# Hybrid decoder layer: the low halves of attention's gate weights made by a negated copy and an accumulating transfer

## What is computed

```python
h = x + 0.5 * swiglu(rmsnorm(x), w_gate_up1, w_down1)
u = rmsnorm(h)
xp | q | k | v | gate_logits = u @ w_in
y_pool = causal_pool_mixer(xp) @ w_branch_pool
y_sb = stick_breaking_attention(q, k, v) @ w_branch_attn
g_pool, g_sb = split(sigmoid(gate_logits))
h = h + (g_pool * y_pool + g_sb * y_sb) @ w_out
h = h + 0.5 * swiglu(rmsnorm(h), w_gate_up2, w_down2)
out = rmsnorm(h)
```

## Time and profile before

| | |
|---|---|
| median of 3 runs | 1924.63 us (1923.79 to 1924.80) |
| profiled execution | 1924.49 us |
| its span in the profile | 1922.5 us |
| PE busy | 1911.0 us (99%) |
| VectorE busy | 1392.9 us (72%) |
| ScalarE busy | 786.7 us (41%) |
| GpSimd busy | 152.1 us (8%) |
| granted TensorE clock | full throughout |

### The profile page before, as it was taken

How to read it: one execution, slowest core, us unless ns; L and a number is a source line. 1 busy time by engine, 2 the same in 40 slices (tenths; PEclk the granted TensorE clock), 3 DMA queues, 4 the chain that set the end, 5 groups by cost and what they waited for, 6 DMA issues and landing times.

```text
span 1922.5 us, 25204 instructions
## 1 busy us (share of the span) xinstructions
PE 1911.0 (99%) x9046; PEld 1599.3 (83%) x9046; DVE 1392.9 (72%) x1714; ACT 786.7 (41%) x1170; POOL 152.1 (8%) x221
## 2 busy tenths in 40 slices
PE   9999999999999999999999999999999999999998
PEld 9888888888888888888888888898888888888886
DVE  6977867774566776786878878879777777755655
ACT  7423232323434543345665652464323232334344
POOL 1000000000000300002443420010000000000002
PEclk9999999999999999999999999999999999999999
DMA  5456654558676534248446347643545444677665
GB/s 165 147 198 228 225 174 149 189 196 312 210 236 196 185 110 151 73 134 236 142 127 175 105 154 254 191 136 114 182 141 197 148 168 153 220 265 240 204 195 200
DMA packets 246723, 347.19 MB, mean 181 GB/s; under 512 B 16368, under 2 KB 150256, under 8 KB 243056
## 3 DMA queue, kind: packets, MB, share of 16 engines
q1 hardware_dynamic: 246640, 346.10, 55.3%
HBM read 232.79 MB, written 112.98 MB: 180 GB/s over the span
## 4 chain that ended last, share of the span: by engine, by line
PE 95%; DVE 2%; DMA 1%; ACT 1%; issue 1%; POOL 1%; SPq 0%; POOLq 0%; DVEq 0%; ACTq 0%
PE bank L1233 39%; PE bank L1330 10%; PE bank L1277 8%; PE bank L1278 8%; PE bank L1279 8%; PE bank L1187 5%; PE bank L1471 4%; PE bank L1379 2%; PE bank L1407 2%; PE bank L1437 2%; PE bank L1543 2%; PE bank L1162 1%; PE bank L1562 1%; PE bank L1561 1%; PE bank L1528 1%; PE bank L1526 1%
## 5 line engine op out<-in xcount | busy, mean ns | idle before, releaser
L2171 DVE TENSOR_TENSOR dn_lo<-dn_lo_raw,dn_hi 128x1024 fp32r<-128x1024 f32 x149 | 181.9, 1223 | 150.9 <-ACT dn_hi L1741 150.5
L1233 PE MATMUL bank<-lo_t,wa_hi 128*128 128x512 f32 x640 | 249.0, 389 | 0.0
L1233 PE MATMUL bank<-hi_t,wa_hi 128*128 128x512 f32 x640 | 249.0, 389 | 0.0
L1233 PE MATMUL bank<-hi_t,wa_lo 128*128 128x512 f32 x640 | 249.0, 389 | 0.0
L1741 ACT ACTIVATE dn_hi<-dn_lo_raw 128x1024 fp32r<-128x1024 f32 x149 | 157.9, 1060 | 219.3 <-DMA dn_lo_raw<-act_dram 219.3
L1277 PE MATMUL bank<-dn_hi 128*128 128x512 f32 x596 | 232.5, 390 | 0.0
L1279 PE MATMUL bank<-dn_lo,dn_hi 128*128 128x512 f32 x596 | 231.9, 389 | 0.0
L1278 PE MATMUL bank<-dn_hi,dn_lo 128*128 128x512 f32 x596 | 231.9, 389 | 0.0
L1233 PE MATMUL bank<-hi_b,wa_hi 128*128 128x512 f32 x480 | 186.9, 389 | 0.9 <-DVE up L2295 0.9
L1233 PE MATMUL bank<-lo_b,wa_hi 128*128 128x512 f32 x480 | 186.8, 389 | 0.0
L1233 PE MATMUL bank<-hi_b,wa_lo 128*128 128x512 f32 x480 | 186.7, 389 | 0.0
(11 more groups left out here) (275 smaller groups left out, 3764.1 us busy)
## 6 DMA issues: line engine op xcount, KB each, us to landing
wa_lo_raw<-in_ffn_w_gate_up_dram SPq DMA_DIRECT2D x87, 512.0 KB, 4.9
dn_lo_raw<-act_dram SPq DMA_DIRECT2D x149, 256.0 KB, 4.3
act_dram<-g SPq DMA_DIRECT2D x44, 512.0 KB, 4.3
wd_t<-in_ffn_w_down_dram SPq DMA_DIRECT2D x44, 512.0 KB, 6.6
act_dram<-s_of SPq DMA_DIRECT2D x88, 256.0 KB, 6.4
wd_dram<-wd_t SPq DMA_DIRECT2D x22, 1024.0 KB, 5.9
dn_lo_raw<-wd_dram SPq DMA_DIRECT2D x85, 256.0 KB, 3.4
dn_lo_raw<-in_ffn_w_down_dram SPq DMA_DIRECT2D x64, 256.0 KB, 3.1
```

The lines of the kernel that those rows point to most:

```text
L1233: last = nc.tensor.matmul(acc, lhs, rhs, start=n == 0 and i != 2 and i < 5, stop=n == 11, skip_group_check=True)
L2171: return nc.vector.tensor_tensor(dst, raw, hi.bitcast(f32), ALU.subtract)
```

## The change

ScalarE makes, right after each high half, the negated high half: a copy of the raw weights with scale -1 into `w_lo`, which is rounded in the same way. When the fourth piece of a unit is done, GpSimd issues one transfer of the whole unit, 128 by 2048 elements or 1 MB, from `w_raw` onto `w_lo`, with addition as its accumulating operation, so that `w_lo` becomes raw less high. Its completion raises `wsum` by 16. VectorE's 28 subtractions go. PE waits at the third matmul of a unit for `wsum` (unit 0 still for `wlo`), and SP waits for `wsum` before it loads over `w_raw`, one step later than before. `wghi` and `wglo`, of the pool's group weights, become one semaphore; no instruction moves by that. `lows_before` counts the low halves that VectorE still makes.

```diff
+def lows_before(g):
+    return min(g, U_GATE + 1) + max(g - U_C, 0)
...
                 if gg >= 2:
                     sp_.wait_ge(whi, gg - 1)
-                    sp_.wait_ge(wlo, gg - 1)
+                    if U_GATE < gg - 2 < U_C:
+                        sp_.wait_ge(wsum, 16 * (gg - 2 - U_GATE))
+                    else:
+                        sp_.wait_ge(wlo, lows_before(gg - 1))
...
-                    for j, piece in PIECES_AT[s - 2] if s > 1 else ():
+                    for j, piece in PIECES_AT[s - 3] if s > 2 else ():
...
                     if m == 2 and fb == GATE_FIRST[j]:
-                        pe.wait_ge(wlo, U_GATE + j + 1)
+                        if j:
+                            pe.wait_ge(wsum, 16 * j)
+                        else:
+                            pe.wait_ge(wlo, U_GATE + 1)
...
                 ab, kts = 2 * piece // PIECES, slice(KT // 2 * (piece % 2), KT // 2 * (piece % 2 + 1))
-                nc.scalar.activation(w_hi[:, par, ab, kts, :], w_raw[:, par, ab, kts, :],
-                                     ACT.Copy).then_inc(whi if piece == PIECES - 1 else wpiece, 1)
+                nc.scalar.activation(w_hi[:, par, ab, kts, :], w_raw[:, par, ab, kts, :], ACT.Copy)
+                last = nc.scalar.activation(w_lo[:, par, ab, kts, :], w_raw[:, par, ab, kts, :], ACT.Copy, scale=-1.0)
+                if piece == PIECES - 1:
+                    last.then_inc(whi, 1)
...
-                for j, piece in PIECES_AT[s - 1] if s else ():
-                    split_piece(j, piece)
...
+            def add_weights(j):
+                par = j % 2
+                pool.wait_ge(whi, U_GATE + j + 1)
+                if j > 1:
+                    pool.wait_ge(wsum, 16 * (j - 1))
+                nc.gpsimd.dma_start(w_lo[:, par].rearrange("p a k f -> p (a k f)").bitcast(f32),
+                                    w_raw[:, par].rearrange("p a k f -> p (a k f)"), accum_op=ALU.add).then_inc(wsum, 16)
+
             for s in range(NA + DRAIN):
+                for j, piece in PIECES_AT[s - 1] if s >= 1 else ():
+                    if piece == PIECES - 1:
+                        add_weights(j)
                 if s < NA:
                     mask_diagonal(s)
```

More of the change, by code:

```diff
@@ L459, in macaron_layer @@
         wlo = sem("wlo")
-        wpiece = sem("wpiece")
-        wghi = sem("wghi")
-        wglo = sem("wglo")
+        wsum = sem("wsum")
+        wg_split = sem("wg_split")
         mb_in = sem("mb_in")
@@ L1027, in load_branch_unit @@
                 sp_.wait_ge(whi, g - 1)
-                sp_.wait_ge(wlo, g - 1)
+                if n < 2:
+                    sp_.wait_ge(wsum, 16 * (g - 2 - U_GATE))
+                else:
+                    sp_.wait_ge(wlo, lows_before(g - 1))
                 for k in range(0, BR, 2):
@@ L1104, in _ @@
             sp_.wait_ge(whi, U_C + 1)
-            sp_.wait_ge(wlo, U_C + 1)
+            sp_.wait_ge(wlo, lows_before(U_C + 1))
             for b in range(2):
@@ L1388, in group_quad @@
                 pe.wait_ge(ylo, 2 * m + 2)
-                pe.wait_ge(wglo, 1)
+                pe.wait_ge(wg_split, 2)
                 for b in range(4):
@@ L1591, in branch_tile @@
                 pe.wait_ge(whi, U_C + j + 1)
-                pe.wait_ge(wlo, U_C + j + 1)
+                pe.wait_ge(wlo, lows_before(U_C + j + 1))
                 for th in (1, 0) if j == 0 else (0, 1):
@@ L2028, in _ @@
             act.wait_ge(mb_add, 5 * NM)
-            nc.scalar.activation(wg_hi[:, :, :], wg_raw[:, :, :], ACT.Copy).then_inc(wghi, 1)
+            nc.scalar.activation(wg_hi[:, :, :], wg_raw[:, :, :], ACT.Copy).then_inc(wg_split, 1)
             pool_hi(0, 1)
@@ L2706, in group_weights_lo @@
             def group_weights_lo():
-                dve.wait_ge(wghi, 1)
+                dve.wait_ge(wg_split, 1)
                 nc.vector.tensor_tensor(wg_lo[:, :, :].rearrange("p g d -> p (g d)"),
@@ L2711, in group_weights_lo @@
                                         wg_hi[:, :, :].rearrange("p g d -> p (g d)").bitcast(f32),
-                                        ALU.subtract).then_inc(wglo, 1)
+                                        ALU.subtract).then_inc(wg_split, 1)
             def pool_weight_sums(u):
@@ L2881, in turned_lo @@
                                             at_hi[:, kbs, c0:c0 + P].bitcast(f32), ALU.subtract).then_inc(alo, 1)
[L2883 to L2894, removed]
             for s in range(NA + DRAIN):
```

## The result

| | before | after |
|---|---|---|
| median, us | 1924.53 (1923.79 to 1925.33) | 1929.61 (1927.37 to 1930.48) |
| executions | 13 | 13 |
| ratio, 95% interval | | 1.0025 (1.0016 to 1.0033) |
| profiled execution, us | 1924.49 | 1929.00 |
| its span, us | 1922.5 | 1927.2 |

The changed kernel is slower by 5.1 us, a ratio of 1.0025. The forecast was 1927.0 us and no change that can be told; the time lies inside the range of 1923 to 1940, but 2.6 us above the forecast and just past the 0.2% that divides "no change" from "slower", which the interval still includes. The mechanism came as forecast at one place, and a second place was missed. When the changed kernel was timed again (e7), one execution of twelve ran at a mean granted clock of 0.752 and took 2386.57 us; it is left out of the median given there.

What follows compares the result with a forecast made beforehand. The prediction took TensorE (PE), busy 1911.0 of 1922.5 us, as the bound. From 1924.49 us, less 0.4 for VectorE, plus 0 for ScalarE and 2.75 for unit 7's wait, it reached 1926.84, given as 1927.0; range 1923.0 to 1940.0.

Steps and rivals of the forecast that it cites:

- What bounds it, and what is removed: Attention stage: PE bounds and waits only 1.28 us; removing VectorE's 28 subtractions gives back 0.4 us.
- ScalarE's copies at 0: ScalarE's 28 negated copies add 0.53 us each, but idle time or other work hides them: cost 0.
- The transfer's length: Accumulating 1 MB transfer from GpSimd's queue: 6.0 us as a plain one plus 2.4 for the second operand, 8.4 us.
- Unit 7: At unit 7 the lead time is 5.65 us against 8.4 us of transfer, so PE waits 2.75 us.
- Units 1 to 6 at nothing: At the six other units lead times of 8.66 us or more cover the transfer, so PE waits nothing.
- Slow transfer: Rival: sums landing from 9.3 us on make several units wait and the kernel slower, 1939.4 us at 12.0; chance 0.34.
- Starved descriptors: Rival: GpSimd can't write the transfer's descriptors while VectorE runs, so sums come after 10.97 us; 1933.0 us, chance 0.10.
- Hidden: Rival: the transfer takes under 5.65 us and PE never waits for it; 1923.4 to 1924.2 us, chance 0.14.
- The sign: Whole kernel: no change that can be told, within 0.2% or 3.85 us, 0.52; slower 0.44, faster 0.04.

Runs made afterwards that it cites:

- e1: The changed kernel without its seven transfers, and with nobody waiting for one; 1924.57 us, ratio 1.0003.
- e4: The changed kernel with plain transfers in place of accumulating ones, same queue, size, source and target; 1924.69 us, ratio 1.0003.
- e5: The changed kernel with four transfers of 256 KB a unit, each as soon as ScalarE has made its piece; 1925.31 us, ratio 1.0005.
- e9: As e5, but GpSimd issues the additions of units 1 to 6 behind the step's masks, not ahead; 1926.16 us, ratio 1.0012.

## Why the prediction was right, and where it was wrong

- **What bounds it, and what is removed:** right in kind. PE gained almost nothing from VectorE's 28 instructions. The place of the earlier trace rows gave back 0.19 to 0.20 us, where 0.4 was taken.
- **ScalarE's copies at 0:** right as a sum, wrong in one place. At unit 2 the piece at 928.56 of the earlier trace rows had no idle time behind it: `at_hi` started 0.57 us after it before, and starts 1.04 us after it now (the piece's high half is at 929.84). VectorE's low half and its scan follow `at_hi`, and PE's transposes step by 0.26 us. ScalarE there, before and in the changed kernel:

```profile
929.13 0.28 ACT L2092 ACTIVATE at_hi<-bank 128x128 fp32r<-128x128 f32 x1
```

```profile
930.36 0.63 ACT L2129 ACTIVATE w_lo<-w_raw 128x512 fp32r<-128x512 f32 x1
930.88 0.28 ACT L2107 ACTIVATE at_hi<-bank 128x128 fp32r<-128x128 f32 x1
```

  That ate the 0.2 us that VectorE gave back, which is why e1 shows no gain. "Nearly every piece is followed by idle time" was read from a few places; the piece that PE's chain ran through was the one to look at.
- **The transfer's length:** right. Taken as 6.0 + 2.4 = 8.4 us; measured 8.0, and its parts are 5.4 plain and 2.6 for the addition, one less and one more than taken. The fit in the Trainium skill, "DMA: Bandwidth & Descriptors", section "Anatomy of one DMA — SWDGE (gpsimd) path", gave 4.4 us for the plain megabyte; e4 measured 5.4. The estimate made from that page with 2 MB read, 6.8, was low as well. Here the measurement decides.
- **Unit 7:** right, and so close by some luck. The lead of 5.65 us stood; the issue came 0.30 us behind the last copy (1100.63 + 0.64 to 1101.57), which the sum had left out, and the landing was 0.4 us shorter than taken. PE's start stepped by 2.69 us against 2.75 forecast.
- **Units 1 to 6 at nothing:** wrong at unit 5, and this is the step that failed. The prediction gave every unit the same landing and compared leads; unit 5 had the longest, 11.78 us, and so looked safest. But the order of the step puts GpSimd's masks, which wait for ScalarE, ahead of the issue (0.9 us: the copy ends at 1039.76, the issue is at 1040.67), and SP issues the loads of a whole head just ahead of it: landing 12.3 us, together 13.2, a wait of 1.43. The prediction weighed SP's neighbours at unit 7 alone. Unit 4, whose sum is issued ahead of the same loads, did not wait. With this term, at 1.4 + 0.1, and with nothing net for VectorE, the same sum reads 1924.49 + 2.85 + 1.53 + 0.14 = 1929.0 against 1929.61 measured; the 0.6 left is inside the interval.
- **The rivals.** *Slow transfer:* its threshold of 9.3 us was passed once in seven, by sharing and not by the addition's rate, so the price of 1939 us at 12 us everywhere was far off. *Starved descriptors:* not seen; with VectorE's scans around them the six sums other than unit 5's landed within 8.8 us. The trap of the Trainium skill, "SBUF — State Buffer", section "SBUF: two separate sides", did not spring here; by its section "Who interferes with whom" it should not, and these landings agree. *Hidden:* no; of the forms with the addition e5 came nearest, 1925.31 us.
- **The sign:** "no change that can be told" was the likeliest single side, with 0.52. At 1.0025 (1.0016 to 1.0033) the time went just past the boundary, by the one missed term: without its 1.5 us it would be 1928.1, 0.18% above the median.

## What to carry to other kernels

When a transfer replaces an engine's work, its lead time must be compared with its landing at each place by itself, and for each place it must be looked up what other queues issue in those microseconds and in which order: the place with the longest lead was one of the two that waited, with six loads issued ahead of its sum, and a place with the same loads behind its sum did not. Cutting the transfer into pieces that start as soon as their part is ready took away one wait and most of the other, at the price of issues on an engine that has work due itself; moving the producer earlier turned the wait into another one, because the producer was on a second chain. Before reading meaning into a step of a microsecond, profile the unchanged kernel twice.

## What the runs showed of the hardware that was not expected

- An accumulating transfer of 1 MB within the chip, issued by GpSimd, lands in a median of 8.0 us and a plain one in 5.4; its issue takes GpSimd 0.88 us against 0.60.
- Behind six loads of 256 KB that another queue has just issued, the accumulating one takes 12.3 us (11.2 to 12.3 in three profiles) and the plain one 11.3, within that range: the 2.6 us of the addition do not show there.
- Ahead of the same six loads they take 8.8 and 5.4 us, and it is the loads that land later (in the changed kernel the pair of `k_hi` in 8.7 us against 3.8).
- A quarter of the size is not a quarter of the time: 256 KB with addition landed in a median of 4.8 us in e5 and 3.5 in e9 (3.3 to 9.9).
- The first logits of attention, which wait for a head's load, moved by up to 1.4 us among eleven profiles, two of them of the same unaltered kernel, 0.69 us apart.
